# A two-block transformer layer on one core: the order in which the feed-forward's second pass fetches its stored partial results

## What is computed

```python
def swiglu(h, w_gate_up, w_down):
    gu = h @ w_gate_up
    gate, up = jnp.split(gu, 2, axis=-1)
    return (jax.nn.silu(gate) * up) @ w_down

x = x + swiglu(rmsnorm(x, norm2_w), w_gate_up, w_down)
return rmsnorm(x, final_norm_w)
```

## Time and profile before

| | us |
|---|---|
| median of three runs (2544.4 to 2554.51) | 2547.93 |
| span of the profiled execution | 2553.6 |
| TensorE busy in it | 2418.7 (95%) |
| VectorE busy | 1469.5 (58%) |
| ScalarE busy | 691.3 (27%) |
| GpSimd busy | 277.6 (11%) |

### The profile page before, as it was taken

One profiled execution on the slowest core, in us unless ns is written; L12 is line 12 of the kernel. 1 busy time (PEld: TensorE's weight loads), 2 busy tenths in 40 slices (PEclk: granted clock), 3 DMA queues, 4 the chain that ended last, 5 costly groups with the idle time before them and its releaser, 6 DMA issues.

```text
span 2553.6 us, 36068 instructions
## 1 busy us (share of the span) xinstructions
PE 2418.7 (95%) x14874; PEld 2011.4 (79%) x14874; DVE 1469.5 (58%) x2428; ACT 691.3 (27%) x1082; POOL 277.6 (11%) x107
## 2 busy tenths in 40 slices
PE   6899999999999999999999999899999989999998
PEld 6778888887788878887787887777888867777777
DVE  6884138883689624051623543664666647676767
ACT  4211111214322103140423326430344421112113
POOL 2100223240000032201200000001000000000000
PEclk8989999999999999999999999999999999999999
DMA  7545544235457742422332352113155552424342
GB/s 270 155 140 165 172 117 137 83 116 172 164 174 234 223 156 100 173 87 77 116 119 86 129 171 77 52 69 136 42 198 194 189 207 83 164 100 147 118 146 91
DMA packets 274799, 354.29 MB, mean 139 GB/s; under 512 B 34673, under 2 KB 169810, under 8 KB 274642
## 3 DMA queue, kind: packets, MB, share of 16 engines
q1 hardware_dynamic: 242242, 303.66, 36.0%
q10 hardware_dynamic: 32400, 48.38, 5.2%
HBM read 247.03 MB, written 104.96 MB: 138 GB/s over the span
## 4 chain that ended last, share of the span: by engine, by line
PE 72%; DVE 13%; DMA 6%; ACT 4%; issue 4%; SPq 1%; POOL 0%; ACTq 0%; DVEq 0%; POOLq 0%
PE PS L502 25%; PE PS L505 16%; PE PS L3214 12%; PE PS L3294 5%; DMA LE<-spill_d 2%; DVE X L3428 1%; DVE W_LO L411 1%; PE PS L1856 1%; PE PS L1836 1%; DMA LAR<-ret_d 1%; PE PS L684 1%; PE PS L2423 1%; PE PS L2418 1%; PE PS L1176 1%; DMA CB<-pch_d 1%
## 5 line engine op out<-in xcount | busy, mean ns | idle before, releaser
L502 PE MATMUL PS<-W_HI,OP_HI 128*128 128x512 f32 (+1 forms) x1184 | 309.2, 405 | 5.3 <-DVE XI L1460 2.9
L444 POOL TENSOR_SCALAR W_HI<-RAW 128x2048 fp32r<-128x2048 f32 (+1 forms) x66 | 132.3, 2014 | 1495.1 <-PE PS L502 671.5
L502 PE MATMUL PS<-W_LO,OP_HI 128*128 128x512 f32 (+1 forms) x1184 | 289.1, 387 | 0.0
L502 PE MATMUL PS<-W_HI,OP_LO 128*128 128x512 f32 (+1 forms) x1184 | 286.8, 384 | 0.0
L502 PEld LDWEIGHTS PS<-W_HI,OP_HI 128*128 128x128 f32 x1184 | 221.2, 196 | 52.7 <-issue 4.5
L502 PEld LDWEIGHTS PS<-W_LO,OP_HI 128*128 128x128 f32 x1184 | 221.3, 190 | 45.6 <-issue 0.3
L502 PEld LDWEIGHTS PS<-W_HI,OP_LO 128*128 128x128 f32 x1184 | 218.7, 188 | 43.9 <-issue 0.5
L531 ACT ACTIVATE OST<-PS 128x512 f32<-128x512 f32 (+2 forms) x164 | 91.1, 556 | 501.6 <-PE PS L505 268.8
L505 PE MATMUL PS<-OP_HI,W_HI 128*128 128x512 f32 (+1 forms) x768 | 191.0, 392 | 3.6 <-POOL W_HI L444 3.6
L505 PE MATMUL PS<-OP_HI,W_LO 128*128 128x512 f32 (+1 forms) x768 | 184.2, 382 | 0.3 <-DVE W_LO L411 0.3
L505 PE MATMUL PS<-OP_LO,W_HI 128*128 128x512 f32 (+1 forms) x768 | 184.0, 382 | 0.2 <-DVE OP_LO L669 0.2
(11 more groups left out here) (502 smaller groups left out, 3784.5 us busy)
## 6 DMA issues: line engine op xcount, KB each, us to landing
RAW<-in_w_gate_up SPq DMA_DIRECT2D x88, 512.0 KB, 5.6
RAW<-in_w_in SPq DMA_DIRECT2D x28, 1024.0 KB, 5.8
RAW<-in_w_out SPq DMA_DIRECT2D x12, 1024.0 KB, 9.2
RAWD<-in_w_down SPq DMA_DIRECT2D x11, 1024.0 KB, 8.4
LE<-spill_d SPq DMA_DIRECT2D x22, 512.0 KB, 8.5
X<-x_d SPq DMA_DIRECT2D x4, 2048.0 KB, 9.2
x_d<-X SPq DMA_DIRECT2D x2, 4096.0 KB, 16.3
ptok_d<-OST ACTq DMA_DIRECT2D x24, 256.0 KB, 2.0
```

What stands on the lines that cost most here:

```text
L444: nc.gpsimd.tensor_scalar(hi, raw, 1.0, 1.0, ALU.mult, ALU.mult).then_inc(*w_hi.by(1))
L502: ins = nc.tensor.matmul(PS[:, bank, 0:width], act_part[:, k, (g.tile0 + a) * P:(g.tile0 + a + 1) * P], w_part[:, slot, k, 0:width], start ...
```

## The change

Only the order of SP's queue in `sp_ffn` changes, and with it some waits. No instruction is added or removed.

- **In each second-pass step** the four fetches of the partial results for the next step move ahead of the loads of the gate/up weights (`load_half` twice). Before, they stood behind them, and behind the wait for `ff_lo(region_no(j+1, 2))`.
- **At the hand-over from the first pass to the second** the four fetches for step 0 are put together, right behind the wait for the sixth product of the last first-pass step, ahead of `load_down(0)` and of that step's stores of PRE. Each waits for the stores of its kind up to the step before (32·i) and no more for all of them (16·NF = 352); the wait for all stands ahead of the second pass.

```diff
@@ -3159,15 +3159,15 @@
+            if i == FFB - 1:
+                sp.wait_ge(*products_done(i, 6))
+                for kind, tile in ((E_GATE, LE2), (E_UP, LE1), (UP1, LUP), (GATE2, LGS)):
+                    sp.wait_ge(*ff_st[kind](32 * i))
+                    fetch(kind, 0, tile)
+                load_down(0)
             for f in range(2):
                 sp.wait_ge(*ff_q(4 * i + 1 + f))
                 store(E_UP, i, f, PRE)
-            if i == FFB - 1:
-                sp.wait_ge(*products_done(i, 6))
-                load_down(0)
-                for kind, tile in ((E_UP, LE1), (UP1, LUP)):
-                    sp.wait_ge(*ff_st[kind](16 * NF))
-                    fetch(kind, 0, tile)
...
-        for kind, tile in ((GATE2, LGS), (E_GATE, LE2)):
-            sp.wait_ge(*ff_st[kind](16 * NF))
-            fetch(kind, 0, tile)
         sp.wait_ge(*ff_lo(region_no(FFB, 2)))
         load_half(FFB + 1, 0)
+        for kind in range(4):
+            sp.wait_ge(*ff_st[kind](16 * NF))
         for i in range(FFB):
...
-            if j + 2 < STEPS:
-                sp.wait_ge(*ff_lo(region_no(j + 1, 2)))
-                load_half(j + 2, 0)
-                load_half(j + 2, 1)
             if i + 1 < FFB:
                 sp.wait_ge(*ff_alo(4 * i + 2))
...
                 fetch(E_GATE, i + 1, LE2)
+            if j + 2 < STEPS:
+                sp.wait_ge(*ff_lo(region_no(j + 1, 2)))
+                load_half(j + 2, 0)
+                load_half(j + 2, 1)
```

## The result

| | before | changed |
|---|---|---|
| median | 2548.47 us (4 runs, 2544.4 to 2554.51) | 2508.18 us (4 runs, 2505.16 to 2514.01) |
| ratio, with 95% interval | 1 | 0.9839 (0.9822 to 0.9857) |
| span of the profiled execution | 2553.6 | 2503.3 |

The changed kernel is 40.3 us faster. The forecast was 2503.8 us, a gain of 44.1, in a range of 2495 to 2514.

The account below looks back on a forecast made before the run. TensorE, busy for 95% of the span, was taken as the bound, losing time to late fetches. Gains of 32.7 us (steps 1 to 9) and 11.4 (step 0) sum to 44.1; 2547.9 − 44.1 = 2503.8 us, range 2495 to 2514.

Parts of the forecast that it names:

- Steps 1 to 9 at 38.07 us: Second-pass steps 1 to 9 run at TensorE's full rate of 168 matmuls each, without stalls; gain 32.7 us.
- step 10 as the picture of the changed steps: Last second-pass step already fetches early and shows no gap; every changed step should look like it.
- Step 0 at 40.4 us: First second-pass step shortens from 51.78 us, with RAWD landing late behind the fetches; gain 11.4 us.
- The RAW loads cost nothing: Gate/up weight loads, moved behind the fetches in second-pass steps, keep over 25 us of cover against 7.4 to land.
- VectorE's slack: At piece 4 of L3294 in step 10, the addition of piece 0 finishes 0.3 us early, the step's thinnest slack.
- VectorE did not become the bound: Rival, steps 1 to 9: VectorE's thin slack costs about 1 us each, gain 35, about 2513 us; chance 0.08.
- The fetch not being the cause: Rival: another late release keeps steps near 42 us, only step 0 gains, about 2538 us; chance 0.04.
- the weights becoming the wait: Rival: RAW loads behind the fetches stall VectorE's sums in each step, 2557 us or more; chance 0.02, shared with clock.
- TensorE's clock did not fall without pauses: Rival: TensorE without pauses gets less clock, 0.89 in every step to eat the gain; counted within the weights' 0.02.

Follow-up runs that it names:

- experiment 1: Kernel before with only the fetches inside second-pass steps moved ahead of the RAW loads, old hand-over kept; 2520.91 us against 2551.07, ratio 0.9889.
- experiment 4: Changed kernel, but the fetches also wait for the old late trigger of the RAW loads, still ahead of them in the queue; 2512.66 us, ratio 0.9843.
- experiment 3: Changed kernel with RAWD's load put ahead of the four fetches at the hand-over; 2508.31 us, ratio 0.9836.
- experiment 2: Kernel before with only the hand-over changed, RAW loads still ahead of the fetches inside the steps; 2542.32 us, ratio 0.9963.
- experiment 5: Changed kernel with each step's RAW loads issued behind the next step's load of RAWD; one run, 2505.52 us.
- experiment 6: Changed kernel with each step's RAW loads issued behind the first two fetches of the next step; one run, 2563.23 us.
- experiment 7: Changed kernel with one unused addition of 128x512 more on VectorE in each second-pass step; one run, 2515.14 us.
- experiment 8: Changed kernel with three more unused, chained additions on VectorE in each second-pass step; one run, 2535.68 us.

## Why the prediction was right, and where it was off

- **The cause in steps 1 to 9.** The fetches stood behind 2 MB of RAW loads. Shown by experiment 1 (the order alone gives 32.6 us) and, finer, by experiment 4: the place in the queue does it, with the old trigger.
- **The cause in step 0.** The prediction took step 0's 51.78 us as it found them and did not say why it was the longest. The rows under experiment 1 do: two fetches waited for the last stores to land. The size of this gain did not need the cause, since it was reckoned from what the changed step would take.
- **Steps 1 to 9 at 38.07 us.** Measured 38.08, the gain 32.6 against 32.7. Taking TensorE's rate from an unbroken stretch, and step 10 as the picture of the changed steps, gave the number to a tenth of a us.
- **Step 0 at 40.4 us.** Measured 40.19, RAWD's landing 9.2 us after its issue where 9.6 was worked out, L3484 at T + 10.73 against T + 10.9. Experiment 3 shows the mechanism. The rule of the Trainium skill (page "DMA: Bandwidth & Descriptors", section "Queues, rings and completion order") that a completion increment lands only behind every earlier write of its DMA engine agrees with the traces: RAWD landed 9.2 us after its issue behind 2 MB, and 4.9 us after it ahead of them. The estimate by the formula in that page's section "Anatomy of one DMA" (3 MB in 9.2 us) was too short: from the first fetch at 2067.71 to RAWD's landing at 2078.91 it took 11.2. The page gives this formula for a single DMA issued from GpSimd, and here SP issued five in a row; the prediction did not say so, and rightly went by the rows. By the profile's bounds step 0 was to lie from 38.07 to 42.15; the same hand-over gave 38.49 to 40.19, by TensorE's own wait ahead of it (the table of experiment 2), a dependence that the prediction did not see. That the profile of the changed kernel came within 0.2 us of the forecast is therefore in part luck.
- **The RAW loads cost nothing.** Right. They go out at T − 3.7 where T − 4.7 was said; 8.7 us more are free (experiment 5), 20 us are not (experiment 6). There loads that came 4.8 us late cost 6.3 us a step, more than the one for one that the prediction set.
- **VectorE's slack.** The step was right and its size not: 0.3 us was reckoned to the start of the matmul, but the weight load comes first and waits for the addition too. In step 10 of the kernel before:

```profile
2528.44 0.41 PEld L3294 LDWEIGHTS PS<-WD_HI,A_HI 128*128 128x128 f32 x2
2528.66 0.61 PE L3294 MATMUL PS<-WD_HI,A_HI 128*128 128x512 f32 x2
```

  With the addition done at 2528.3 that leaves 0.1 us, near the 0.14 that experiments 7 and 8 give. As the change adds no work to VectorE, this did not matter for the time. Nor did a wrong reading beside it: 28.37 of 42.20 us is 67% of the step for VectorE, and not 55% or less.
- **The end result, 2508.2 against 2503.8.** The stretch gained 44.2 us, as forecast (44.1); the medians moved 40.3, with an interval of about 36 to 45. Behind the stretch nothing moved: 46.7 us from the last step's T to the end, in both kernels. Ahead of it the same instructions of TensorE took 2079.8 us in one profile and 2073.7 in the other, so the two profiled spans differ by 50.3 us. The prediction took its range from the spread of the runs, but set the profiled execution's gain against the median as if the part ahead stood still. It does not: the feed-forward starts anywhere from 1830.2 to 1841.8 us. That this scatter is also what lies between 44.1 and 40.3 is argued, not shown, since the other runs have no trace.
- **Rivals.** VectorE did not become the bound: in steps 2 to 9 TensorE is busy all the time. The fetch not being the cause fell with experiment 1; the weights becoming the wait needed experiment 6's order; TensorE's clock did not fall without pauses, it was 1.00 over 304.70 us.

## What to carry to other kernels

When loads of two kinds share a queue, order them by when they are read, not by when they are wanted out of the way: the small urgent one first, the large one with 25 us of cover behind. Where an engine's waits point at a DMA, ask what was issued just ahead of it before asking for an earlier trigger. And look for one iteration of the loop that already runs in the new order (here the last, which had no more weights to load): its rows give the changed step to a tenth of a us.

## What the runs showed of the hardware

- Gaps of the same length had two outcomes for TensorE's clock. In the kernel before, step 1 has a gap of 2.19 us and a mean clock of 0.96, while step 5 has one of 2.16 and a clock of 1.00, and is 1.07 us shorter (41.08 against 42.15 us). The same holds for longer ones: a gap of 3.13 us went with 0.96 in step 9 of the kernel before, and one of 3.12 with 1.00 in step 7 of experiment 2, where the step took 42.08 us instead of 43.10. A gap of 1.73 us in every step left it at 1.00 (experiment 8), gaps of 3.7 to 5.6 us gave 0.92 to 0.96 (experiment 6). Windows of step 5 before, of a step of experiment 8 and of one of experiment 6:

```profile
2297.10:2338.20 41.10, 38.68 (x169) 31.38 (x169) 28.27 (x37) 7.95 (x11) 1.92 (x1) 1.00 0.37 128
```
```profile
2124.10:2164.20 40.10, 38.37 (x169) 31.45 (x168) 30.35 (x40) 7.95 (x11) 1.93 (x1) 1.00 0.37 123
```
```profile
2115.30:2159.90 44.60, 40.77 (x170) 33.20 (x169) 28.65 (x37) 7.95 (x11) 1.92 (x1) 0.92 0.34 118
```

  Experiment 6's steps cost 6.3 us more for loads that came 4.8 us late on the mean (43.5 us in nine waits); the clock is a likely part of the difference. What tells the two outcomes apart stays open.
- A PSUM bank had to be given back about 0.2 us before the matmul's place, since the weight load ahead of it (0.22 us earlier in an unbroken row) was held too: 0.14 and 0.15 us of slack in experiments 7 and 8, where the matmul's start alone gave 0.3.
- A stop of TensorE cost about 0.3 us more than its idle time in the profile: 2.02 us for 1.73 (experiment 8), 0.47 for 0.15 (experiment 7), 2.11 for two stops of 1.55 together (step 0 of the changed kernel). Part of it is how idle time is counted: in an unbroken row the matmuls overlap, each lasting 0.39 us and the next starting 0.227 behind it.
- 1 MB took 4.9 us from issue to landing with nothing ahead (experiment 3) and 8.8 to 9.8 behind 2 MB of fetches (the other kernels with the changed hand-over); the fetches of 512 KB took 3.5 to 6.4 us in the changed kernel, and up to 10.8 behind 2 MB of RAW loads.
